# The last feed-forward group by token chunks, and the down projections of the last two groups in one accumulation

## What is computed

```python
h = _rmsnorm(x, norm_ffn_g)
u = jnp.einsum('bsd,df->bsf', h, w_up)                    # 1024 -> 2 * 2816
up = jnp.pad(u, ((0, 0), (1, 1), (0, 0)))
u = up[:, :-2] * conv_w[0] + up[:, 1:-1] * conv_w[1] + up[:, 2:] * conv_w[2] + conv_b
a, b = jnp.split(u, 2, axis=-1)
x = x + jnp.einsum('bsf,fd->bsd', jax.nn.silu(a) * b, w_down)
...
return _rmsnorm(x, final_norm_g)
```

## Time and profile before

| what | value |
|---|---|
| median of three executions | 2540.14 us |
| profiled execution, its own time | 2540.42 us |
| span in its profile | 2537.4 us |
| PE busy, share of the span | 2444.5 us, 96% |
| DVE, ACT, POOL busy, share of the span | 59%, 32%, 36% |

### The profile page before, as it was taken

One profiled execution on the slowest core, in us unless ns is written; L12 is line 12 of the kernel. 1 busy time (PEld: TensorE's weight loads), 2 busy tenths in 40 slices (PEclk: granted clock), 3 DMA queues, 4 the chain that ended last, 5 costly groups with the idle time before them and its releaser, 6 DMA issues.

```text
span 2537.4 us, 34379 instructions
## 1 busy us (share of the span) xinstructions
PE 2444.5 (96%) x12666; PEld 2100.3 (83%) x12666; DVE 1487.6 (59%) x2165; ACT 818.4 (32%) x1466; POOL 915.7 (36%) x1234
## 2 busy tenths in 40 slices
PE   7999999998999989999999999999999999999995
PEld 7999999887888868888888888888888888888883
DVE  7546666687879963343344355555555555555556
ACT  4335555555668851133322211111011111101113
POOL 4453645688767530152400221222122122212214
PEclk9999999999999999999999999999999999999998
DMA  8643434432212062221334500011010001101002
GB/s 306 227 162 139 150 123 163 165 107 91 91 42 81 14 192 91 76 91 67 124 125 134 190 25 33 25 41 33 25 41 25 33 25 41 33 25 41 25 17 99
DMA packets 83376, 224.56 MB, mean 89 GB/s; under 512 B 8000, under 2 KB 43200, under 8 KB 72768
## 3 DMA queue, kind: packets, MB, share of 16 engines
q1 hardware_dynamic: 81968, 222.69, 25.3%
q10 hardware_dynamic: 1296, 0.39, 0.1%
HBM read 174.82 MB, written 48.23 MB: 88 GB/s over the span
## 4 chain that ended last, share of the span: by engine, by line
PE 60%; POOL 1%; DVE 1%; ACT 1%; DMA 0%; issue 0%; SPq 0%; POOLq 0%; ACTq 0%; DVEq 0%
PE r_bank L1630 28%; PE r_bank L1755 14%; PE r_bank L1654 9%; PE r_bank L1685 5%; PE r_bank L1704 1%; PE r_bank L1733 1%; PE r_bank L1667 1%; POOL r_x_rows L1615 0%; PE r_bank L1716 0%; POOL r_last_stat L1619 0%; DMA h_raw<-mix_scratch 0%; POOL r_wxq_lo L1560 0%; SPq L1451 0%; POOL r_wxq_hi L1558 0%; ACT r_x_rows L1853 0%
## 5 line engine op out<-in xcount | busy, mean ns | idle before, releaser
L1940 DVE TENSOR_TENSOR r_x_rows<-r_bank,r_x_rows 128x512 f32<-128x512 f32 x528 | 364.1, 690 | 378.9 <-PE r_bank L1755 378.7
L1630 PE MATMUL r_bank<-r_h_hi,r_w_hi 128*128 128x512 f32 x1056 | 411.0, 389 | 0.0
L1630 PE MATMUL r_bank<-r_h_hi,r_w_lo 128*128 128x512 f32 x1056 | 410.8, 389 | 0.0
L1630 PE MATMUL r_bank<-r_h_lo,r_w_hi 128*128 128x512 f32 x1056 | 410.8, 389 | 0.0
L1597 POOL TENSOR_SCALAR r_w_hi<-r_stage 128x1024 fp32r<-128x1024 f32 x64 | 67.6, 1056 | 842.5 <-PE r_bank L1755 528.9
L802 PE MATMUL t_proj<-t_w_hi,t_hbuf 128*128 128x384 f32 x1056 | 315.8, 350 | 4.1 <-ACT t_nat L944 2.0
L1839 ACT ACTIVATE r_conv<-r_bank,r_tap 128x1536 f32<-128x1536 f32 x44 | 72.0, 1637 | 661.6 <-PE r_bank L1630 661.6
L1630 PEld LDWEIGHTS r_bank<-r_h_hi,r_w_hi 128*128 128x128 f32 x1056 | 198.2, 188 | 41.4
L1630 PEld LDWEIGHTS r_bank<-r_h_hi,r_w_lo 128*128 128x128 f32 x1056 | 198.2, 188 | 41.2
L1630 PEld LDWEIGHTS r_bank<-r_h_lo,r_w_hi 128*128 128x128 f32 x1056 | 198.2, 188 | 41.2
L1755 PE MATMUL r_bank<-r_w_hi,r_g_hi 128*128 128x512 f32 x528 | 210.1, 398 | 18.3 <-DVE r_g_lo L1963 11.0
(11 more groups left out here) (210 smaller groups left out, 5067.9 us busy)
## 6 DMA issues: line engine op xcount, KB each, us to landing
t_hbuf<-split_x SPq DMA_DIRECT2D x60, 1024.0 KB, 4.8
r_stage<-in_w_up_units SPq DMA_DIRECT2D x44, 512.0 KB, 3.3
split_x<-t_hbuf SPq DMA_DIRECT2D x12, 1024.0 KB, 4.9
r_stage<-in_w_down SPq DMA_DIRECT2D x22, 512.0 KB, 3.3
t_stage<-in_w_in_units SPq DMA_DIRECT2D x6, 1536.0 KB, 6.9
t_xkv_raw<-in_w_xkv_heads SPq DMA_DIRECT2D x16, 512.0 KB, 6.1
t_x_raw<-in_x_turned SPq DMA_DIRECT2D x12, 512.0 KB, 8.0
h_raw<-mix_scratch SPq DMA_DIRECT2D x12, 512.0 KB, 7.7
```

The costliest lines, as they stand in the source:

```text
L1630: ins = nc.tensor.matmul(up_bank(s)[:, c * BANK:(c + 1) * BANK], l, r, start=(k == 0 and j == 0), stop=(k == KT - 1 and j == 2))
L1940: nc.vector.tensor_tensor(x[:, t, cols], down_bank(n), x[:, t, cols], ALU.add).then_inc(add_done, 1)
```

## The change

The last group (`LAST` = 21) leaves the common body. Its ups come by token chunks, both halves of a chunk one behind the other, in the order chunk 2 (the sample), chunk 0, chunk 1. No downs are woven between them. The convolution and the product follow chunk by chunk (`END_PARTS`: 512, 384 and 640 tokens; the second stops at token 384, since token 511 needs its neighbour in the next chunk) into new tiles `e_hi`, `e_lo`. POOL splits the last down weights into tiles of their own, `we_hi`, `we_lo`, and so doesn't wait for the downs of group 20. Then the downs of groups 20 and 21 go into one accumulation: six matmuls for each half tile and one add. The tiles come in the order in which their parts are ready, 8 to 11 first. The squares of the final norm are summed by half tiles, and DVE's mean is an addition of the two sums. The tiles of ACT and POOL are now those at even places of the order, the ones of DVE those at odd places.

```diff
 def groups(eng, body):
-    body(0, True, False)
-    with eng.Fori(1, FT - 1) as i:
-        body(i, False, False)
-    body(FT - 1, False, True)
+    body(0, True)
+    with eng.Fori(1, LAST) as i:
+        body(i, False)
...
+LAST = FT - 1
+END_PARTS = [(2, slice(1024, 1536), slice(1024, 1536)), (0, slice(0, 512), slice(0, 384)), (1, slice(512, 1024), slice(384, 1024))]
+END_TILES = [8, 9, 10, 11, 0, 1, 2, 3, 4, 5, 6, 7]
+END_NEEDS = [1, 1, 1, 1, 2, 2, 2, 3, 3, 3, 3, 3]
...
             groups(nc.gpsimd, body)
+            split(LAST, 1, LAST * 3 + 2, False)
+            pool.wait_ge(stage_loaded[2], 16 * FT)
+            pool.wait_ge(end_up, 2)
+            nc.gpsimd.tensor_scalar(we_hi[:, :], stage[2][:, :], 1.0, 1.0, ALU.mult, ALU.mult).then_inc(whi_done, 1)
+            pool.wait_ge(whi_done, LAST * 3 + 3)
+            nc.gpsimd.tensor_tensor(we_lo[:, :], stage[2][:, :], f32(we_hi[:, :]), ALU.subtract).then_inc(end_weights, 1)
...
-            for t in range(NT):
-                pool.wait_ge(last_mean, t + 1)
-                nc.gpsimd.tensor_tensor(last_stat[:, t, 1:2], last_stat[:, t, 0:1], half[:, 0:1], ALU.pow).then_inc(last_rstd, 1)
-                if t % 2 == 0 and t:
-                    apply_gain(t - 1)
-            apply_gain(NT - 1)
+            for m in range(NT):
+                pool.wait_ge(last_mean, m + 1)
+                nc.gpsimd.tensor_tensor(last_stat[:, m, 0:1], last_stat[:, m, 0:1], half[:, 0:1], ALU.pow).then_inc(last_rstd, 1)
+                if m % 2:
+                    apply_gain(m - 1)
...
             groups(nc.tensor, body)
-            for n in range(DOWNS):
-                down(FT - 1, n)
+            for n, (c, _, _) in enumerate(END_PARTS):
+                for s in range(2):
+                    if n == 0:
+                        pe.wait_ge(w_split[s], FT)
+                        pe.wait_ge(conv_done, LAST * 2 + s - 1)
+                    for k in range(KT):
+                        ins = up(s, c, k)
+                    ins.then_inc(end_up, 1)
+            pe.wait_ge(g_split, LAST)
+            pe.wait_ge(w_split[2], LAST)
+            pe.wait_ge(end_weights, 1)
+            for m, t in enumerate(END_TILES):
+                pe.wait_ge(end_split, END_NEEDS[m])
+                for c in range(2):
+                    n = 2 * m + c
+                    pe.wait_ge(add_done, (LAST - 1) * DOWNS + max(n - 1, 0))
+                    cols = slice(c * BANK, (c + 1) * BANK)
+                    for g, (gh, gl, wh, wl) in enumerate(((g_hi, g_lo, w_hi[2], w_lo[2]), (e_hi, e_lo, we_hi, we_lo))):
+                        gh, gl = (z[:, t * P:(t + 1) * P] for z in (gh, gl))
+                        for j, (l, r) in enumerate(((gh, wh), (gh, wl), (gl, wh))):
+                            ins = nc.tensor.matmul(down_bank(n), l, r[:, cols], start=(g == 0 and j == 0), stop=(g == 1 and j == 2))
+                    ins.then_inc(down_done, 1)
...
+            for n, (_, _, cols) in enumerate(END_PARTS):
+                end_in(n, 0)
+                act.wait_ge(end_conv, 2 * n + 1)
+                nc.scalar.activation(conv[:, 0, cols], conv[:, 0, cols], ACT.Silu).then_inc(end_silu, 1)
+                end_in(n, 1)
+                act.wait_ge(end_prod, n + 1)
+                nc.scalar.copy(e_hi[:, cols], conv[:, 0, cols]).then_inc(end_hi, 1)
...
+                for c in range(2):
+                    cols = slice(c * BANK, (c + 1) * BANK)
+                    act.wait_ge(add_done, (LAST - 1) * DOWNS + 2 * m + c + 1)
...
+                    nc.scalar.activation(stage[1][:, cols], x[:, t, cols], ACT.Square, scale=D ** -0.5,
+                                         accum_out=last_stat[:, m, c:c + 1]).then_inc(sum_done, 1)
+                if m % 2:
+                    by_rstd(m - 1)
...
+            def mean(m):
+                dve.wait_ge(sum_done, 2 * m + 2)
+                nc.vector.scalar_tensor_tensor(last_stat[:, m, 0:1], last_stat[:, m, 0:1], EPS, last_stat[:, m, 1:2],
+                                               ALU.add, ALU.add).then_inc(last_mean, 1)
...
+            for n, (_, _, cols) in enumerate(END_PARTS):
+                for s in range(2):
+                    end_shifts(n, s)
+                dve.wait_ge(end_silu, n + 1)
+                dve.wait_ge(end_conv, 2 * n + 2)
+                nc.vector.tensor_tensor(conv[:, 0, cols], conv[:, 0, cols], conv[:, 1, cols], ALU.mult).then_inc(end_prod, 1)
+                dve.wait_ge(end_hi, n + 1)
+                nc.vector.tensor_tensor(e_lo[:, cols], conv[:, 0, cols], f32(e_hi[:, cols]), ALU.subtract).then_inc(end_split, 1)
+            for m in range(NT):
+                last_add(2 * m)
+                if m:
+                    mean(m - 1)
+                last_add(2 * m + 1)
+                if m >= 3 and m % 2:
+                    scale(m - 2)
             mean(NT - 1)
-            scale(NT - 2)
+            scale(NT - 1)
```

More of the change, by code:

```diff
@@ L1519, in load, with body @@
                 sp.dma_start(stage[s][:, :], src).then_inc(stage_loaded[s], 16)
-            def body(i, first, last):
+            def body(i, first):
                 if not first:
                     load(i, 1, False)
-                if not last:
-                    load(i + 1, 0, False)
+                load(i + 1, 0, False)
                 load(i, 2, first)
@@ L1631, in up @@
                                            stop=(k == KT - 1 and j == 2))
-                if c == CH - 1 and k == KT - 1:
-                    ins.then_inc(up_done, 1)
+                return ins
             for _, kind, what in order["PE"]:
@@ L1741, in _ @@
                     for k in range(KT):
-                        up(0, 0, c, k, True, False)
+                        up(0, c, k)
             def down(i, n):
@@ L1771, in body @@
                         pe.wait_ge(h_done, both)
-                    up(i, s, c, k, first, last)
+                    ins = up(s, c, k)
+                    if c == CH - 1 and k == KT - 1:
+                        ins.then_inc(up_done, 1)
             groups(nc.tensor, body)
-            for n in range(DOWNS):
-                down(FT - 1, n)
+            for n, (c, _, _) in enumerate(END_PARTS):
[4 more added lines that the diff above has]
+                    for k in range(KT):
+                        ins = up(s, c, k)
+                    ins.then_inc(end_up, 1)
+            pe.wait_ge(g_split, LAST)
+            pe.wait_ge(w_split[2], LAST)
+            pe.wait_ge(end_weights, 1)
+            for m, t in enumerate(END_TILES):
+                pe.wait_ge(end_split, END_NEEDS[m])
[8 more added lines that the diff above has]
+                    ins.then_inc(down_done, 1)
         @block.scalar
@@ L1968, in _, with end_shifts @@
             groups(nc.vector, body)
-            def mean(t):
-                dve.wait_ge(sum_done, t + 1)
-                nc.vector.tensor_scalar(last_stat[:, t, 0:1], last_stat[:, t, 0:1], 1.0 / D, EPS, ALU.mult, ALU.add).then_inc(last_mean, 1)
-            def scale(t):
-                if t == 0:
+            nc.vector.tensor_copy(tap[:, :, :], taps[:, :, :, LAST]).then_inc(tap_set, 1)
+            dve.wait_ge(tap_set, FT)
+            def end_shifts(n, s):
+                dve.wait_ge(end_mid, 2 * n + s + 1)
+                for z, (j, o, x_cols) in enumerate(END_SHIFTS[n]):
+                    if z:
+                        dve.wait_ge(end_step, 2 * n + s + 1)
+                    nc.vector.scalar_tensor_tensor(conv[:, s, o], up_bank(s)[:, x_cols], tap[:, j, s:s + 1], conv[:, s, o],
+                                                   ALU.mult, ALU.add).then_inc(end_conv if z else end_step, 1)
@@ L1976, in scale @@
+            def scale(m):
+                if m == 1:
                     dve.wait_ge(last_gain, 16)
-                dve.wait_ge(last_rstd, t + 1)
-                nc.vector.scalar_tensor_tensor(x[:, t, :], x[:, t, :], last_stat[:, t, 1:2], stage[0][:, :], ALU.mult,
+                t = END_TILES[m]
+                dve.wait_ge(last_rstd, m + 1)
+                nc.vector.scalar_tensor_tensor(x[:, t, :], x[:, t, :], last_stat[:, m, 0:1], stage[0][:, :], ALU.mult,
                                                ALU.mult).then_inc(out_a, 1)
-            for t in range(NT):
-                add(FT - 1, 2 * t)
-                if t:
-                    mean(t - 1)
-                add(FT - 1, 2 * t + 1)
-                if t >= 2 and t % 2 == 0:
-                    scale(t - 2)
+            for n, (_, _, cols) in enumerate(END_PARTS):
[6 more added lines that the diff above has]
+                nc.vector.tensor_tensor(e_lo[:, cols], conv[:, 0, cols], f32(e_hi[:, cols]), ALU.subtract).then_inc(end_split, 1)
```

57 lines of the change are left out of this document (36 added, 21 removed).

## The result

The changed kernel took 2518.8 to 2521.47 us in four executions, median 2519.57, against 2540.21 (2539.67 to 2540.84) for the kernel before, run beside it: a ratio of 0.992, 95% interval 0.9903 to 0.9937. That is 0.8% faster; 2520.0 was forecast.

The account below looks back on a forecast made before the run. POOL's turn with ACT and DVE, not PE, was taken to set the tail. From 2435.56, 65.3 us of matmuls plus waits, clock, last tile and exit gave a 2517.3 us span, hence 2520.0 us; range 2516 to 2525.

Parts of the forecast that it names:

- Both holes of the old tail: After the last ups: PE waits 10.96 us for the last group's convolution, then on POOL's turns in the final norm.
- new wait 1, POOL's split: Among the last group's ups, PE waits 1.2 us for POOL to split the weights of half 1.
- new wait 2, DVE's order: Before the third half tile of joined downs, PE waits 2.85 us, as DVE does all convolution parts before the first add.
- the clock behind it: After the wait for DVE's first add, the clock falls to 1.2 GHz for 8 matmuls, losing 1.6 us.
- DVE's scaling between adds: In the joined downs, a scaling between two adds on DVE costs PE 0.15 us per pair, four times, 0.6 us.
- last matmul to last write: Last tile's add, squares, mean, power, then POOL's gain and DVE's scaling one after the other: together 6.7 us.
- last write to end: At the end of the span, the last transfer and the exit take 3.5 us.
- upper end of 2522.5: Top of the forecast's own range, 2517.5 to 2522.5 us, said to come from the bounds of DVE's wait and clock.
- POOL and DVE did not fall out of step: Rival, 10%: in the tail, scalings start inside gains and PE waits 1.1 us more in five pairs; 2525.4 us.
- the rival of a clock that stays low: Rival, 2%: the clock stays low through the joined downs, 144 matmuls at 0.2 us more; 2547 us, slower.
- the shorter end: Rival, 7%: no clock fall and a 2.0 us wait for DVE give 2517.5 us; an earlier last scaling, 2516.5.
- The transfers out: Rival, 2%: the tail stays bound by something unseen, such as the output transfers, and nothing is won.

Follow-up runs that it names:

- the one with the shorter wait: Against the changed kernel, only the first add goes ahead, between the product and the rest of the third part; median 2516.87 us, ratio 0.9908.
- the run with half 0 first: Against the changed kernel, PE makes half 0 of the first two parts before half 1 of the first; median 2518.5 us, ratio 0.992.
- the repetition: The changed kernel measured once more, with nothing changed; median 2519.34 us, ratio 0.992 to the kernel before.
- two small moves: Against the changed kernel, first two adds ahead of the third part's rest, and half 0 of two parts first; together median 2513.48 us, ratio 0.9896.

## Why the prediction was right

**Both holes of the old tail were idle time of PE, and both went.** The two half changes show each: without chunks PE waits 10.9 us as in the earlier trace rows, without joined downs the tail is 40 us long from its first add, as long as in the kernel before. Alone the chunks give 4.1 us as first built and 7.0 with the third part earlier (101.8 to 94.8), the joined downs 13.1 (to 88.7), together 19.8: nearly the sum of the last two.

**The terms.** From the start of group 21 to the end of the span the sum gave 81.7 us; measured are 82.0.

| step | forecast, us | measured, us |
|---|---|---|
| new wait 1, POOL's split | 1.2 | 1.17 |
| new wait 2, DVE's order | 2.85 | 2.96 |
| the clock behind it | 1.6, 8 matmuls | some 1.5, 7 matmuls |
| DVE's scaling between adds | 0.15 in 4 pairs | 0.19 in 4 pairs |
| last matmul to last write | 6.7 | 6.0 |
| last write to end | 3.5 | 3.7 |

With the 65.3 us of matmuls the measured column adds up to 81.4. Most of what is missing to 82.0 are the restarts: around the first wait PE lost 1.45 us and not 1.17, around the second 3.12 and not 2.96, by the distances between its starts. The sum had no term for that. Wait 2 is longer than forecast mostly because ACT's middle tap of 512 tokens took 0.78 us, where I had 0.65 from an instruction of another form.

The small waits of the pairs are no entry in a list of waits. They are seen in the distance between starts, here in the changed kernel, 0.33 and 0.31 in place of 0.23 us:

```profile
2501.00 0.39 PE L1812 MATMUL r_bank<-r_we_hi,r_e_lo 128*128 128x512 f32 x1
2501.33 0.47 PE L1812 MATMUL r_bank<-r_w_hi,r_g_hi 128*128 128x512 f32 x1
2501.64 0.40 PE L1812 MATMUL r_bank<-r_w_lo,r_g_hi 128*128 128x512 f32 x1
2501.87 0.39 PE L1812 MATMUL r_bank<-r_w_hi,r_g_lo 128*128 128x512 f32 x1
```

Three causes are shown, not argued: wait 2 by the two runs with adds ahead, its clock by the one with the shorter wait, wait 1 by the run with half 0 first. The last tile was put 0.7 us too high: gain and scaling at 3.7 us one after the other, which took 3.4 (2512.56 to 2515.98), and what lies ahead of them at 3.0, which took 2.6 (from 2509.97). That excess made up for the missing restarts and the longer exit, so the sum is closer than its terms, by luck. The forecast's own upper end of 2522.5 doesn't follow from the bounds that it names: 3.6 us for wait 2 gives 2520.8.

**Where two errors met.** The span was forecast at 2517.3 and came out at 2519.7 in the first profile and 2518.2 in the repetition; the start of group 21 was 2.1 and 0.5 us later than in the profile of before, by differences that arose far ahead of the change. On the other side, an execution's own time was 1.8 us above its span in the changed kernel (2521.47 and 2519.7) where it was 3.0 before, and I had added 3.0. That row is an extreme one: over 44 later executions of the kernel before, time less span was 1.76 to 2.96 us, median 2.05, and over the 9 of the changed kernel 1.76 to 1.84. All kernels with joined downs stay at 1.74 to 1.84, the two without reach 2.25 and 2.04. That the median came within 0.5 us of the forecast is in part luck. What makes this difference was not tried and stays open.

**The rivals.** POOL and DVE did not fall out of step: a gain ended 0.7 us ahead of the scaling behind it (2504.27 and 2504.95), and the five scalings before the last took 1.27 to 1.28 us each. The mean with two inputs was held up, as that rival feared, by up to 0.54 us. It cost PE nothing: the held mean ended at 2504.28, and the add behind it started at 2504.34, when its half tile was done. With one input it was not (0.14 us). The Trainium skill, GPSIMD Engine Reference, section 1, says that POOL contends with DVE instructions that have two SBUF inputs; the runs agree (0.69 and 3.37 us beside a gain, against 0.15 and 1.28 alone). It names those in a 2-port mode as well, of which no run here tells. The clock fell once and did not stay low. Two windows of the joined downs behind it:

```profile
2483.00:2488.00 5.00, 5.00 (x24) 4.14 (x23) 3.12 (x7) 3.47 (x9) 3.47 (x3) 1.00 0.04 12
...
2503.00:2508.00 5.00, 5.00 (x23) 3.88 (x22) 4.53 (x7) 3.43 (x8) 2.84 (x4) 1.00 0.45 182
```

PE is busy throughout at 1.00, so the rival of a clock that stays low did not occur. Nor did the shorter end: wait 2 was above 2.85 us, and the last scaling started 0.05 us behind the gain, not ahead of it. The transfers out didn't take over as the limit: two adds ahead in DVE's order shortened the whole by 3.9 us.

**What the change had of no use.** The tile order and the halves of the squares are worth nothing in this kernel, and the order on DVE and on POOL left 5.4 us that two small moves won back.

## What to carry to other kernels

- A hole at the end of a loop can be filled with work that was hidden elsewhere: matmuls that were woven in without need are worth most where PE would else wait for others. Look at what limits the tail with and without them; here 2.7 us of PE per pair met a turn of 5.1 to 5.5 us through the other engines, and doubling PE's share made the turn free.
- When work moves to parts, write down for each engine what stands ahead of the first instruction that frees a buffer. Two adds in the wrong place cost 3.9 us, wait and clock together.
- At the very end, order the last transfers by who is done first; two that are issued together cost 1.3 us here.
